# Loading attention operands: value tiles over 128 rows, a head's loads spread over its groups, and the first head loaded from GpSimd's queue during the projection

## The reference, cut to what matters

```python
proj = _rms_norm(h, pre_norm_g[l]) @ w_in[l]
u_rwkv, g_rwkv, q_sb, k_sb, v_sb, g_sb, merge_logits = _split(proj, IN_SIZES)
# stick breaking attention, 16 heads of 64 channels, strictly causal
logits = einsum("bhqd,bhkd->bhqk", q, k) * 64 ** -0.5
log_keep = where(visible, log_sigmoid(-logits), 0.0)
log_between = cumsum(log_keep, axis=3, reverse=True) - log_keep
weights = where(visible, exp(log_sigmoid(logits) + log_between), 0.0)
o_sb = einsum("bhqk,bhkd->bhqd", weights, v)
y_sb = o_sb * silu(g_sb)
```

## Time and profile before

| | us |
|---|---|
| median of 3 runs | 4376.24 (4373.36 to 4381.48) |
| the profiled execution's own time | 4379.16 |
| its span in the profile | 4377.4 |
| projection, from 0 to the barrier | about 2026 |
| attention | about 2026 to 3104 |
| recurrence and output | about 3104 to 4377 |
| PE busy over the span | 4171.0 (95%) |
| DVE, ACT, POOL busy over the span | 2380.5, 1666.2, 804.4 |

### The profile page before, as it was taken

The page is one execution under the profiler, slowest core; times in us unless marked ns, Lnnn a source line. Parts: engine busy times, 40 slices in busy tenths (PEclk is TensorE's granted clock), DMA queues, the critical chain, the costliest instruction groups (busy, mean ns, idle before and its releaser), DMA issues. The chain is left out here.

```text
span 4377.4 us, 90822 instructions
## 1 busy us (share of the span) xinstructions
PE 4171.0 (95%) x35784; PEld 3344.7 (76%) x35784; DVE 2380.5 (54%) x3103; ACT 1666.2 (38%) x3296; POOL 804.4 (18%) x637
## 2 busy tenths in 40 slices
PE   7999999997999999997999999999899999999999
PEld 7888888985888888885555555655688888878887
DVE  5444444443444444442777777777467766743222
ACT  4222222223222222222666666666444444421111
POOL 2110111111111111110000000000256666610222
PEclk9999999998999999998999999999899999999999
DMA  2333433333333333334443442442233333355653
GB/s 93 109 117 119 122 109 110 102 115 110 109 118 116 109 104 118 107 103 113 89 94 69 82 93 63 87 94 62 75 114 99 101 104 100 92 184 177 189 188 129
DMA packets 486971, 479.74 MB, mean 110 GB/s; under 512 B 260610, under 2 KB 370818, under 8 KB 480914
## 3 DMA queue, kind: packets, MB, share of 16 engines
q1 hardware_dynamic: 475154, 450.33, 37.1%
q10 hardware_dynamic: 11520, 25.17, 1.6%
HBM read 305.45 MB, written 169.93 MB: 109 GB/s over the span
## 5 line engine op out<-in xcount | busy, mean ns | idle before, releaser
L1210 DVE TENSOR_TENSOR_SCAN kept<-keep,kept 128x512 f32<-128x512 f32 (+1 forms) x448 | 436.6, 975 | 63.1 <-ACT keep L1172 22.6
L1172 ACT ACTIVATE keep<-z 128x512 f32<-128x512 f32 (+3 forms) x704 | 343.4, 506 | 302.4 <-PE z L1105 242.1
L1636 POOL TENSOR_TENSOR off<-NT,tri 128x512 f32<-128x512 f32 x165 | 206.1, 1276 | 1181.6 <-ACT NT L1540 1181.6
L1115 PE MATMUL turned<-t_identity,kept 128*128 128x128 f32 (+1 forms) x2432 | 383.0, 280 | 38.6 <-DVE kept L1210 38.6
L1115 PEld LDWEIGHTS turned<-t_identity,kept 128*128 128x128 f32 (+1 forms) x2432 | 280.7, 136 | 154.9 <-DVE kept L1210 50.0
L1182 ACT COPY w<-turned 128x512 f32<-128x512 f32 (+4 forms) x704 | 363.2, 528 | 92.4 <-PE turned L1115 90.7
L1207 DVE TENSOR_TENSOR_SCAN kept<-keep,hidden 128x512 f32<-128x512 f32 (+3 forms) x256 | 284.2, 1116 | 156.3 <-ACT keep L1172 155.7
L1104 PE MATMUL z<-k_high,q_parts 128*128 128x512 f32 (+3 forms) x704 | 308.6, 439 | 36.1 <-DMA k_low<-scr_k_lo 27.9
L1142 PE MATMUL acc<-w,dv 128*64 128x512 f32 (+3 forms) x1280 | 322.8, 562 | 15.4 <-issue 15.4
L1104 PEld LDWEIGHTS z<-k_high,q_parts 128*128 128x128 f32 x704 | 137.8, 196 | 191.5 <-ACT keep L1172 107.6
L1105 PE MATMUL z<-k_low,q_parts 128*128 128x512 f32 (+3 forms) x704 | 256.6, 368 | 0.0
(11 more groups left out here) (554 smaller groups left out, 10688.4 us busy)
## 6 DMA issues: line engine op xcount, KB each, us to landing
w_raw0A<-in_w_main SPq DMA_DIRECT2D x42, 512.0 KB, 3.9
w_raw0B<-in_w_main SPq DMA_DIRECT2D x42, 512.0 KB, 3.9
w_raw1A<-in_w_main SPq DMA_DIRECT2D x41, 512.0 KB, 4.0
w_raw1B<-in_w_main SPq DMA_DIRECT2D x41, 512.0 KB, 3.8
KB<-scr_kb SPq DMA_DIRECT2D x33, 512.0 KB, 5.2
AR<-scr_ar SPq DMA_DIRECT2D x33, 512.0 KB, 5.4
y_raw<-scr_y SPq DMA_DIRECT2D x64, 256.0 KB, 4.5
merge<-scr_merge SPq DMA_DIRECT2D x64, 256.0 KB, 6.3
```

The lines of the kernel that those rows point to most:

```text
L1115: mm = pe.transpose(turned[num % TB][0:size, P * r:P * r + P], kept[kept_in(g)][:, src:src + size], t["identity"][:, :])
L1172: act.activation(keep[num % KB][:, 0:size], z[num % ZB][:, 0:size], ACT.Sigmoid, scale=-DH ** -0.5).then_inc(keep_done, 1)
L1210: dve.tensor_tensor_scan(dst, data, data, kept[kept_in(g)][:, end:end + 1], ALU.mult, ALU.bypass).then_inc(scanned, 1)
L1636: pool.tensor_tensor(out, a, b, op).then_inc(s[name], 1)
```

## The change: what it does

1. `dv_diag` is loaded over all 128 partitions (the row 127 too, with the rows of `dv`), and the row from `v_edge` is written over partition 127 afterwards. For heads 1 to 15 this second transfer is issued by POOL, which waits for the first (`diag_in`); PE waits for it (`edge_in`).
2. A head's loads are no longer issued together. `due_after(g)` gives the parts by turn: high keys of the odd head after turn 0, its low keys and dv after turn 1, its dv_diag after turn 2; queries and high keys of the next even head after turn 3, its low keys and dv after turn 4, its dv_diag after turn 5; the queries of the next odd head after turn 7 (of head 1 after group 0). The store of y_sb and the gate of group g+2 stay ahead of them.
3. Head 0 and the mask are loaded whole by POOL's queue behind its last `value_steps` of the projection's last pass (`first_head_loader`), under semaphores that the barrier's release doesn't clear. For this the attention's tiles are laid out before the projection, and the projection's tiles in another order, so that head 0's tiles lie over projection tiles whose last use is before that point. `FIRST_PARTS` is gone: PE waits for all of head 0 at once.
4. POOL clears w[0], w[5] and the meta slot of dv[1] at the attention's start, in place of both dv slots and all eight w; the meta slot of dv[0] is cleared in the projection.

```diff
...
@@ -82,17 +82,17 @@
...
+        mix = [sb(f"mix{x}", [P, N]) for x in "rkv"]
+        run, rate = sb("run", [P, N]), sb("rate", [P, N])
+        keep, grow = sb("keep", [P, NCG, CHUNK + 1]), sb("grow", [P, NCG, CHUNK])
+        unit, gain = sb("unit", [P, N]), sb("gain", [P, N])
+        lora = sb("lora", [P, N])
         w_raw = [sb(f"w_raw{b}", [P, KC, P]) for b in range(2)]
         w_hi = [sb(f"w_hi{b}", [P, KC, P], F32R) for b in range(2)]
         w_lo = [sb(f"w_lo{b}", [P, KC, P], F32R) for b in range(2)]
...
@@ -857,6 +857,11 @@
                     scaled_units(k, g, at, size)
                 for g, (at, size) in enumerate(SG):
                     value_steps(k, g, at, size)
+            if first_head is not None:
+                now(pool, logits_pe, PAIRS - 1, G - 1)
+                now(pool, vt_pe, PAIRS - 1, G - 1)
+                now(pool, bonus_done, PAIRS - 1, G - 1)
+                first_head(pool)
...
@@ -951,40 +956,79 @@
...
+KB, WB = 4, 8
+
+
+def attention_tiles(nc):
+
...
+        sb = lambda name, shape, dt=F32: ctx.enter_context(nc.sbuf_tensor(name, shape, dt))
+        a = {"kept": [sb(f"kept{b}", [P, shortest if b >= 2 else longest]) for b in range(4)]}
+        a["keep"] = [sb(f"keep{b}", [P, 512]) for b in range(2)]
+        a.update(q_parts=[], k_high=[], k_low=[], dv=[], dv_diag=[])
+        for b in range(2):
+            a["q_parts"].append(sb(f"q_parts{b}", [P, SEQ], F32R))
+            a["k_high"].append(sb(f"k_high{b}", [P, META + SEQ], F32R))
+            a["k_low"].append(sb(f"k_low{b}", [P, META + SEQ], F32R))
+            a["dv"].append(sb(f"dv{b}", [P, 1 + QT, DH]))
+            a["dv_diag"].append(sb(f"dv_diag{b}", [P, QT, DH]))
+            if b == 0:
+                a["hidden"] = sb("hidden", [P, 512])
+        a["keep"] += [sb(f"keep{b}", [P, 512]) for b in range(2, KB)]
+        a["w"] = [sb(f"w{b}", [P, 512]) for b in range(WB)]
+        a["low_half"], a["total"] = sb("low_half", [DH, 512]), sb("total", [DH, 512])
+        a["gate"], a["y"] = [sb(f"gate{b}", [DH, 512]) for b in range(2)], [sb(f"y_sb{b}", [DH, 512]) for b in range(2)]
+    return a
...
+FIRST = namedtuple("First", "const_in zeroed queries keys steps diagonal edges")
+
+
+def first_head_loader(io, scratch, a, head0):
+
+    def load(pool):
+        rows = slice(0, DH)
+        pool.memset(a["dv"][0][:, 0, :], 0.0).then_inc(head0.zeroed, 1)
+        pool.dma_start(a["q_parts"][0][0:DH, :].bitcast(F32), scratch["q_hi"][rows, :]).then_inc(head0.queries, 16)
+        pool.dma_start(a["q_parts"][0][DH:P, :].bitcast(F32), scratch["q_lo"][rows, :]).then_inc(head0.queries, 16)
+        for tile, name in ((a["k_high"][0], "k_hi"), (a["k_low"][0], "k_lo")):
+            for part in (slice(0, DH), slice(DH, P)):
+                pool.dma_start(tile[part, :].bitcast(F32), scratch[name][rows, PAD:TOK]).then_inc(head0.keys, 16)
+        by_tile = scratch["dv"][CHUNK:TOK, rows].rearrange("(k p) c -> p k c", p=P)
+        pool.dma_start(a["dv_diag"][0][:, :, :], by_tile).then_inc(head0.diagonal, 16)
+        pool.wait_ge(head0.zeroed, 1)
+        pool.dma_start(a["dv"][0][0:META, 0, :], scratch["dv"][PAD:CHUNK, rows]).then_inc(head0.steps, 16)
+        pool.dma_start(a["dv"][0][:, 1:, :], by_tile).then_inc(head0.steps, 16)
+        pool.dma_start(a["hidden"][:, :], io["hidden"]).then_inc(head0.const_in, 16)
+        pool.wait_ge(head0.diagonal, 16)
+        edge = scratch["v_edge"][:, rows].rearrange("(o k) c -> o k c", o=1)
+        pool.dma_start(a["dv_diag"][0][P - 1:P, :, :], edge).then_inc(head0.edges, 16)
+
+    return load
+
+
+def attention_phase(nc, sem, t, io, scratch, a, head0):
 
...
-    LAG, ZB, TB, KB, WB = 3, 2, 4, 4, 8
-    FIRST_PARTS = [(0, GROUP), (GROUP, 2 * GROUP), (2 * GROUP, QT)]
+    LAG, ZB, TB = 3, 2, 4
...
-        const_in, cleared = sem("a_const_in"), sem("a_cleared")
-        qk_first, v_first = [[sem(f"a_{x}_first{b}") for b in range(len(FIRST_PARTS))] for x in ("qk", "v")]
+        cleared = sem("a_cleared")
+        edge_in, diag_in = [sem(f"a_edge_in{b}") for b in range(2)], [sem(f"a_diag_in{b}") for b in range(2)]
...
@@ -1023,29 +1067,41 @@
...
+        def due_after(g):
+
+            pair, turn = divmod(g, 2 * GROUPS)
+            even, odd = 2 * pair + 2, 2 * pair + 1
+            if g == 0:
+                return [(odd, "queries"), (odd, "high")]
+            plan = {0: [(odd, "high")], 1: [(odd, "low"), (odd, "steps")], 2: [(odd, "diagonal")],
+                    3: [(even, "queries"), (even, "high")], 4: [(even, "low"), (even, "steps")], 5: [(even, "diagonal")],
+                    7: [(odd + 2, "queries")]}
+            return [(head, what) for head, what in plan.get(turn, []) if head < HEADS]
+
         @block.sync
         def _(sp):
...
+            def load_queries(head, done):
+                u, rows = head % 2, slice(DH * head, DH * head + DH)
+                sp.dma_start(q_parts[u][0:DH, :].bitcast(F32), scratch["q_hi"][rows, :]).then_inc(done, 16)
+                sp.dma_start(q_parts[u][DH:P, :].bitcast(F32), scratch["q_lo"][rows, :]).then_inc(done, 16)
+
+            def load_keys(head, dst, name, done):
+                u, rows = head % 2, slice(DH * head, DH * head + DH)
+                for part in (slice(0, DH), slice(DH, P)):
+                    sp.dma_start(dst[u][part, :].bitcast(F32), scratch[name][rows, PAD:TOK]).then_inc(done, 16)
+
+            def load_steps(head, done):
+                u, rows = head % 2, slice(DH * head, DH * head + DH)
                 by_tile = scratch["dv"][CHUNK:TOK, rows].rearrange("(k p) c -> p k c", p=P)
...
+                if head == 1:
+                    sp.wait_ge(cleared, 3)
+                sp.dma_start(dv[u][0:META, 0, :], scratch["dv"][PAD:CHUNK, rows]).then_inc(done, 16)
+                sp.dma_start(dv[u][:, 1:, :], by_tile).then_inc(done, 16)
+
+            def load_diagonal(head, done):
+                u, rows = head % 2, slice(DH * head, DH * head + DH)
+                by_tile = scratch["dv"][CHUNK:TOK, rows].rearrange("(k p) c -> p k c", p=P)
+                sp.dma_start(dv_diag[u][:, :, :], by_tile).then_inc(done, 16)
 
...
@@ -1055,9 +1111,6 @@
...
-            sp.dma_start(hidden[:, :], io["hidden"]).then_inc(const_in, 16)
-            for p, (first, last) in enumerate(FIRST_PARTS):
-                load(0, first, last, qk_first[p], v_first[p])
             load_gate(0)
             load_gate(1)
             for g in range(GROUPS_ALL):
@@ -1065,12 +1118,18 @@
...
                     load_gate(g + 2)
-                if g % (2 * GROUPS) == 0:
-                    head = head_of(g) + 1
-                    load(head, 0, QT, qk_in[head % 2], v_in[head % 2])
-                if g % (2 * GROUPS) == GROUPS - 1 and head_of(g) + 2 < HEADS:
-                    head = head_of(g) + 2
-                    load(head, 0, QT, qk_in[head % 2], v_in[head % 2])
+                for head, what in due_after(g):
+                    qk, v = qk_in[head % 2], v_in[head % 2]
+                    if what == "queries":
+                        load_queries(head, qk)
+                    elif what == "high":
+                        load_keys(head, k_high, "k_hi", qk)
+                    elif what == "low":
+                        load_keys(head, k_low, "k_lo", qk)
+                    elif what == "steps":
+                        load_steps(head, v)
+                    else:
+                        load_diagonal(head, diag_in[head % 2])
...
@@ -1083,16 +1142,19 @@
             def queries_and_keys(g):
                 head = head_of(g)
                 if head == 0:
-                    pe.wait_ge(qk_first[min(rank(g), len(FIRST_PARTS) - 1)], 96)
+                    pe.wait_ge(head0.queries, 32)
+                    pe.wait_ge(head0.keys, 64)
                 else:
                     pe.wait_ge(qk_in[head % 2], 96 * loads_of(head))
 
             def value_steps(g):
                 head = head_of(g)
                 if head == 0:
-                    pe.wait_ge(v_first[min(rank(g), len(FIRST_PARTS) - 1)], 64 if rank(g) == 0 else 48)
+                    pe.wait_ge(head0.steps, 32)
+                    pe.wait_ge(head0.edges, 16)
                 else:
-                    pe.wait_ge(v_in[head % 2], 64 * loads_of(head))
+                    pe.wait_ge(v_in[head % 2], 32 * loads_of(head))
+                    pe.wait_ge(edge_in[head % 2], 16 * loads_of(head))
 
...
@@ -1177,7 +1239,7 @@
...
                     if num == 0:
-                        act.wait_ge(cleared, 2 + WB)
+                        act.wait_ge(cleared, 2)
...
@@ -1221,10 +1283,15 @@
...
-            for tile in dv:
-                pool.memset(tile[:, 0, :], 0.0).then_inc(cleared, 1)
-            for tile in w:
-                pool.memset(tile[:, :], 0.0).then_inc(cleared, 1)
+            pool.memset(w[0][:, :], 0.0).then_inc(cleared, 1)
+            pool.memset(w[5][:, :], 0.0).then_inc(cleared, 1)
```

(45 more changed lines are left out.)

## The result

| | before | after | forecast |
|---|---|---|---|
| median | 4376.98 us (4 runs) | 4328.0 us (4 runs, 4324.03 to 4330.33) | 4287 |
| ratio | | 0.9887, 95% interval [0.987, 0.9904] | 0.9796 |
| span of the profiled execution | 4377.4 us | 4322.2 us | 4287.7 |

Faster, but 41 us slower than forecast, and outside the range (4274 to 4316). The trace puts most of the gap in a place that the prediction did not price. (The profiled execution is the fastest of the four, so the spans differ from the forecast by 34.5 us and the medians by 41.)

A forecast was written before the change was run, and what follows sets the result against it. PE was taken to bound the attention, with DVE next. From 4376.2 us, 32.7 for the opening and 57 for the gate stalls were taken off, giving 4286.5, stated as 4287; own range 4274 to 4298, wider range 4274 to 4316.

The forecast's parts named there:

- Part 1: Attention: with dv_diag over 128 partitions, DVE's seven waits for a gate go, 8.2 us each, 57 us (39 to 63).
- Part 2: Attention's opening, to y_sb of turn 2: head 0 in place at the barrier wins 32.7 us (17.2 to 35.3).
- Part 3: Projection's last pass: POOL's eleven transfers fit in the 48.06 us before the barrier, with no delay and no cost to PE.
- Part 4: Attention: a head's loads issued by turn bring no new wait; the memsets taken away win 0.
- A: Rival: DVE becomes the bound earlier in the attention; stalls give 39, the opening 17.2: 4320 us; chance 0.09.
- B: Rival: POOL comes late to the barrier, 50 us late at 22.4 ns a piece: 4337 us; chance 0.11.
- D: Rival: the gate isn't what holds DVE; the stalls stay while the opening gains: 4343 us; chance 0.03.
- C: Rival: dv_diag over 128 partitions still runs on one engine and holds SP's queue; slower, 4406 us; chance 0.03.

The follow-up runs named there:

- e1: The kernel before with only the projection's tiles put in the changed kernel's order, in both halves: 4411.87 us, ratio 1.008.
- e3: The changed kernel with half A's projection tiles in their old order and, in half B, 960 bytes of padding ahead of w_raw: 4294.42 us, ratio 0.9817.
- e8: The kernel before with SP loading dv_diag over 128 rows and POOL adding the v_edge row; loads neither spread nor moved early: 4302.52 us, ratio 0.9826.
- e10: e3 with SP loading dv_diag over 127 rows and the v_edge row behind it, heads 1 to 15, at the same turns: 4575.29 us.
- e7: The kernel before with 32 bytes of padding between w_hi and w_lo: 4413.52 us.
- e9: The kernel before with 32 bytes of padding behind w_lo in half A; in half B w_hi moved by 32 bytes, w_lo by 256: 4397.28 us.
- e11: The kernel before with 32 bytes of padding between hn_hi and hn_lo, and half B's weight tiles moved by 256 in all: 4398.65 us.
- e6: The kernel before with 32 bytes of padding ahead of hn_hi, so hn_hi, hn_lo and all projection tiles move together: 4379.14 us, ratio 1.0002.

## Why the prediction was wrong

**What failed is a step that the prediction did not take.** The change moves mix, run, rate, keep, grow, unit, gain and lora ahead of w_raw, and no term of the sum stood for it: its passage on PE in the last pass, which ends in "It costs nothing", dealt with the weights' transfers alone, and every other term took the projection to be as long as before. The runs put a loss of 32 us in its place, by the barrier (2059.07 against 2027.04); e1, with nothing else changed, loses 4411.87 - 4375.87 = 36, and e3 wins 34 back from the changed kernel. It couldn't be read from the trace of before, where every weight tile lies a multiple of 256 bytes from the stream; but the diff showed that operands of the busiest engine change their place, and a bound for that belonged in the range.

**Part 1, the seven gate stalls: right.** Forecast 57 us; from y_sb of turn 2 of the first pair to the last y_sb the trace gives 984.4 - 929.2 = 55.2, 7.9 a pair, DVE's end of the two. e8, with the 128 rows alone, has the same pairs, so the cause that the prediction named is the right one. DVE's row, y_sb of turn 2 in two pairs running, 122.50 us apart (forecast near 122, before 130.4):

```profile
2240.03 0.68 DVE L1282 TENSOR_TENSOR y_sb<-total,gate 64x512 f32<-64x512 f32 x1
...
2362.53 0.68 DVE L1282 TENSOR_TENSOR y_sb<-total,gate 64x512 f32<-64x512 f32 x1
```

**Part 2, the opening: right.** Forecast 32.7, measured from the barrier to y_sb of turn 2: 89.2 - 58.5 = 30.7. DVE is busy for 52.51 of the 58.5 us, a share of 0.90 where 0.93 was taken. But it credited the wrong part of the change. e8 wins 22.2 of the 30.7 with SP still loading head 0 behind the barrier; the early load by POOL is worth 8.5 more. The sum of 32.7 doesn't depend on this split; a forecast for the early load alone would have been far too high.

**Part 3, POOL's loads: right in what it concluded, not in how.** POOL takes 21.2 us from its first issue to the edge row (2009.90 to 2031.06), where the bandwidth bound had 43. That bound gave the loads only the free share of the DMA engines at 200 GB/s; the engines ran at a full share and 225 GB/s while the loads moved, and SP's stores stood back for them:

```profile
2010.00:2030.00 20.00, 20.00 (x92) 16.20 (x91) 5.09 (x7) 2.81 (x6) 6.87 (x10) 1.00 1.03 225
```

POOL's eleven issues together hold it for 7.6 us; the estimate from the Trainium skill (DMA: Bandwidth & Descriptors, the anatomy of one DMA on the gpsimd path), 2.0 us each and the bytes over 436 GB/s, gave 32, 11 us more than the trace. The first ten follow each other without a gap, so nothing shows of the up to 9 us by which the prediction feared that DVE's copies would hold them up. SP's stores beside them do wait (one issue of scr_gg holds SP's queue for 7.32 us, where e1 has 0.44), PE doesn't:

```profile
2024.98 7.32 SPq L302 DMA_DIRECT2D scr_gg<-stage2B  x1
```

**Part 4, the loads by turn: right at nothing**, PE waits 1.9 us for keys in the whole stage. By e8 the spread over the turns wins nothing either.

**The rivals.** A (DVE earlier the bound), B (POOL late) and D (the gate isn't what holds DVE) are each refuted by the rows above. C didn't come, as a transfer of 128 rows has a DMA share of 0.67 while it moves. e10 shows what it would have cost: with the loads spread over the turns, a transfer on one engine makes the kernel far slower than C's 4406, and by another wait than C's, PE's for dv_diag and not DVE's for the gate. With the layout repaired the kernel takes 4294.42, 7 us from the forecast, with a span of 4289.3 against 4287.7: the sum over the attention was sound, the list of what the diff changes was not complete.

## What to carry to other kernels

Go through the diff by what each engine reads, and not only by what it waits for: moving a matmul's operands in SBUF is a change to the busiest engine. Where a 512-column stream of fp32r runs against weights of the same type, try both weight tiles and the streams at distances that are multiples of 256 bytes, the only ones that kept the short step here; a pad of a few words decides on 30 us of this kernel. And before restructuring loads, change the one transfer that runs on a single engine by itself: the 128 rows alone gave 75 us (4377.4 - 4302.52), the best version 81 (4375.87 - 4294.42).

## What the runs showed of the hardware that had not been expected

- The step between 512-column fp32r matmuls, each with its own load of weights, depends on where the weights lie to the stream: 227 ns (544 cycles at 2.4 GHz) at distances that are multiples of 256 bytes, 232 to 234 (about 560) at 32, 64, 96 and 128 over. The medians of shorter steps hardly move: 147 ns at 320 columns, 154 at 336, 173 at 384 (174 in the changed kernel, 175 in e7). One weight tile off costs as much as all of them (w_lo in e7, w_hi in e9), hn_lo alone 21.6 us of 30 (e11). The Trainium skill (SBUF — State Buffer, the section on who interferes with whom) says that PE never waits on anyone, and names its two read ports independent; moving the tiles of other engines cost nothing here (e9, half A), but PE's step does depend on where its own two reads lie to each other. That one read holds up the other is an inference; no run shows how they meet. Theory P (a load of weights disturbs the stream beside it) and theory T (all tiles of a block must agree modulo 256) each explain a part of e7 and e11, and neither all.
- The output projections behind the attention stay at 227 in both kernels, with weights and stream both at 32 over a multiple of 64: the remainder that they share doesn't matter, as in e6.
- A DMA over 127 rows of 16 pieces holds the queue that issues the next one for 29 to 34 us at a DMA share of 0.08 to 0.09; the same over 128 rows is issued in 0.58 us and lands in 4.7 (median of the 15 in the changed kernel).
